# Odd mixer of a fused transformer kernel: unscaled queries, scores of one head per bank, output projection between the head pairs

## The chip, the cores and the metric

The kernel runs on one core of one Trainium2 chip. The metric is the device time of one launch in microseconds (us): 1750.55 us, the median of 3 runs (1749.31 to 1753.45). Lower is better.

## The reference

Two transformer blocks follow each other on a sequence of 256 tokens of width 1024, all in float32. The change lies in the last attention layer, the odd mixer of the second block:

```python
def odd_mixer(x, mix_norm, w_qkv, q_norm, k_norm, w_out):
    proj = rms_norm_2(x, mix_norm) @ w_qkv
    q, k, v = jnp.split(proj, [GQA_Q_WIDTH, GQA_Q_WIDTH + GQA_KV_WIDTH], axis=-1)
    q = rms_norm_2(q.reshape(Bsz, S, 16, 64), q_norm)
    k = rms_norm_2(k.reshape(Bsz, S, 4, 64), k_norm)
    v = v.reshape(Bsz, S, 4, 64)
    q = apply_rope(q, cos, sin)
    k = apply_rope(k, cos, sin)
    return gqa_block_attention(q, k, v) @ w_out
```

There are 16 query heads of 64, each four sharing one key and value head. `rms_norm_2` divides each head's 64 values by the root of their mean square and multiplies by a gain; `apply_rope` turns pairs of values by angles that depend on the position. The attention is softmax over all 256 keys. The block's feed-forward layer (stage f below) follows and ends the kernel.

## The kernel before

Five engine programs are written out by hand: `tensor_program` (PE), `scalar_program` (ACT), `vector_program` (DVE), `gpsimd_program` (POOL) and `sync_program` (SP, which issues the weight loads). Each engine works through its instructions in the written order; semaphores (`on.wait_ge`) tie them together. Ten stages follow each other: a, conv, b, c, attn, d, even, e, odd, f. Here only the last two matter: odd, the mixer above, and f, a feed-forward stage.

Weights come as 260 pieces of 128x2048 in one stream. A piece is split into a high part (ACT copies it to `wh`, 5 slots) and a low part (DVE subtracts, into `wl`, 7 slots), so that three matmuls on reduced-precision operands (`mm3`: high by high, low by high, high by low) give a float32 product. `Ring.fill` and `Ring.need` place these splits in the program of ACT and of DVE; p0 is the first piece of a stage. Stage odd has pieces p0 to p0+9: two for keys and values, four for queries, four for the output projection. A piece is given back for reuse when PE signals `multiplied`.

`tensor_program`'s `odd` projects keys and values (`kv_part(t)`, t the half of 128 tokens), then queries (`q_part(j, t)`, j the half of the heads), 24 matmuls of 512 columns each. DVE scales each head by its root (POOL computes it) and turns it (`rope`); PE transposes (`kv_turn`, `q_turn`). Then the shared function `attention` goes over 8 pairs of heads:

```python
for i in range(n_pairs + 3):
    if i < n_pairs:
        scores(i)
    if 2 <= i < n_pairs + 2:
        turn(i - 2)
    if i >= 3:
        values(i - 3)
    if i in beside:
        beside[i]()
```

`scores(i)` fills two PSUM banks, and a step later can refill them only when ACT's exponentials of that pair are through. DVE first scales the pair before (`scale(i - 1)`: reciprocal of the sums, then four multiplications), then takes the maxima of pair i; ACT makes the exponentials, `turn` transposes the probabilities over two banks, ACT copies them to `PTg`, `values` multiplies by the values, and ACT and DVE split the result into `xTh` and `xTl`. After the last pair, `close` runs the output projection, 96 matmuls of 512 columns: all pieces for t = 0, then all for t = 1, with the transposes for stage f (`turn_in`) ahead of the last piece. `seam` adds the result to x (`post_scale`) and multiplies by the next gain (`pre_scale`) on DVE, squares x on ACT, and places a weight split between.

## Time and profile before

| what | value |
|---|---|
| median of 3 runs | 1750.55 us |
| profiled execution | 1749.03 us, of which the span is 1747.6 us |
| mean granted TensorE clock | 0.975 |
| PE busy | 1664.8 us (95%) |
| DVE busy | 974.7 us (56%) |
| ACT busy | 786.6 us (45%) |
| POOL busy | 69.3 us (4%) |

The span begins with the first instruction and ends with the last; 1.4 us lie outside it. All starts below are us from the span's start. The line numbers are those of the kernel before. PEclk in a window is the granted TensorE clock as a share of 2.4 GHz, so 0.50 is 1.2 GHz and 1.00 is 2.4 GHz.

### The profile page before, as it was taken

Reading aid. Unit: us, or ns where it says so; the run is one execution under the profiler, and the core shown is the slowest. Engines: PE = TensorE matmul, PEld = TensorE weight load, DVE = VectorE, ACT = ScalarE, POOL = GpSimd, SP = SyncE. Lnnn points to the kernel's source line nnn. Section 1 sums busy time; section 2 is a strip of 40 time slices with the busy share of each in tenths; the row PEclk is TensorE's granted clock in tenths of the full one; section 3 lists DMA queues with packets and bytes.
Section 4 is the critical chain, followed back from the end, with each engine's and each line's share of the span. In section 5 each row is a group of like instructions: output and inputs, shape, how many; then the busy total and the mean of one; then the engine's idle time right before and its main releaser. Section 6 shows DMA issues by size and latency. Waiting matters only on the chain. (4 is left out here: it accounts for less than half of the span.)

```text
span 1747.6 us, 18630 instructions
## 1 busy us (share of the span) xinstructions
PE 1664.8 (95%) x7938; PEld 1356.6 (78%) x7938; DVE 974.7 (56%) x992; ACT 786.6 (45%) x954; POOL 69.3 (4%) x99
## 2 busy tenths in 40 slices
PE   6999998999999999999999999988999998599999
PEld 5877776788888888897788889765788886378887
DVE  4646675554565445655545468756454557544543
ACT  5444544443453434554434357534343444534442
POOL 1000000100010000000000000100000002000000
PEclk9999998999999999999999999989999999699999
DMA  8545541454455544553555364313354553026451
GB/s 328 187 179 183 190 159 49 182 200 183 183 192 193 193 168 174 206 193 109 182 182 202 145 229 155 134 43 103 133 217 170 198 189 145 1 99 226 182 192 49
DMA packets 51391, 289.33 MB, mean 166 GB/s; under 512 B 14151, under 2 KB 14791, under 8 KB 18026
## 3 DMA queue, kind: packets, MB, share of 16 engines
q1 hardware_dynamic: 50732, 286.84, 44.9%
q8 instruction: 63, 1.03, 0.2%
q10 hardware_dynamic: 576, 1.29, 0.2%
q14 instruction: 20, 0.16, 0.0%
HBM read 287.06 MB, written 1.05 MB: 165 GB/s over the span
## 5 line engine op out<-in xcount | busy, mean ns | idle before, releaser
L1759 DVE TENSOR_TENSOR wl<-raw,wh 128x2048 fp32r<-128x2048 f32 x260 | 588.7, 2286 | 164.2 <-ACT wh L1145 164.2
L516 PE MATMUL ps<-wh,xTh 128*128 128x512 f32 x1408 | 561.3, 399 | 25.5 <-DVE wl L1759 8.3
L516 PE MATMUL ps<-wh,xTl 128*128 128x512 f32 x1408 | 554.4, 394 | 0.0
L516 PE MATMUL ps<-wl,xTh 128*128 128x512 f32 x1408 | 553.9, 393 | 0.0
L1145 ACT ACTIVATE wh<-raw 128x2048 fp32r<-128x2048 f32 x260 | 489.0, 1908 | 4.2 <-PE ps L516 3.0
L516 PEld LDWEIGHTS ps<-wh,xTh 128*128 128x128 f32 x1408 | 268.0, 190 | 91.4 <-issue 9.8
L516 PEld LDWEIGHTS ps<-wh,xTl 128*128 128x128 f32 x1408 | 267.7, 190 | 57.4
L516 PEld LDWEIGHTS ps<-wl,xTh 128*128 128x128 f32 x1408 | 268.1, 190 | 54.3
L2451 POOL TENSOR_SCALAR st<-st 128x1 f32<-128x1 f32 (+2 forms) x46 | 29.8, 648 | 1490.4 <-ACT tmp L1164 852.4
L1208 ACT ACTIVATE sgf<-ps,st 128x256 f32<-128x256 f32 x22 | 10.4, 474 | 104.1 <-PE ps L516 104.1
L1208 ACT ACTIVATE sge<-ps,st 128x256 f32<-128x256 f32 x22 | 10.4, 474 | 98.9 <-PE ps L516 98.9
L516 PE MATMUL ps<-xTh,wh 128*128 128x256 f32 x192 | 54.6, 284 | 0.0
L516 PE MATMUL ps<-xTl,wh 128*128 128x256 f32 x192 | 54.3, 283 | 0.0
L516 PE MATMUL ps<-xTh,wl 128*128 128x256 f32 x192 | 54.3, 283 | 0.0
L1208 ACT ACTIVATE sgd<-ps,st 128x256 f32<-128x256 f32 x22 | 10.4, 473 | 97.2 <-PE ps L516 97.2
L1208 ACT ACTIVATE sgc<-ps,st 128x256 f32<-128x256 f32 x22 | 10.4, 472 | 95.8 <-PE ps L516 95.8
L1208 ACT ACTIVATE sgb<-ps,st 128x256 f32<-128x256 f32 x22 | 10.4, 472 | 93.0 <-PE ps L516 93.0
L1208 ACT ACTIVATE sga<-ps,st 128x256 f32<-128x256 f32 x22 | 10.4, 474 | 91.7 <-PE ps L516 91.7
L1831 DVE SCALAR_TENSOR_TENSOR hbe<-ps,st,sge 128x256 f32<-128x256 f32 x22 | 10.6, 483 | 73.4 <-ACT sge L1208 73.4
L1831 DVE SCALAR_TENSOR_TENSOR hbf<-ps,st,sgf 128x256 f32<-128x256 f32 x22 | 10.6, 483 | 72.8 <-ACT sgf L1208 72.8
L1831 DVE SCALAR_TENSOR_TENSOR hbd<-ps,st,sgd 128x256 f32<-128x256 f32 x22 | 10.6, 483 | 71.3 <-ACT sgd L1208 71.3
L1831 DVE SCALAR_TENSOR_TENSOR hbc<-ps,st,sgc 128x256 f32<-128x256 f32 x22 | 10.6, 484 | 69.7 <-ACT sgc L1208 69.7
(330 smaller groups left out, 2290.2 us busy)
## 6 DMA issues: line engine op xcount, KB each, us to landing
raw<-in_w SPq DMA_DIRECT2D x260, 1024.0 KB, 4.8
gains<-in_rows SPq DMA_DIRECT2D x18, 512.0 KB, 4.6
x<-in_x ACTq DMA_DIRECT2D x2, 512.0 KB, 7.7
nab<-in_rpb SPq DMA_DIRECT2D x32, 32.0 KB, 2.5
out_x<-x SPq DMA_DIRECT2D x2, 512.0 KB, 2.6
qn<-in_rpb SPq DMA_DIRECT2D x16, 32.0 KB, 2.5
xd<-in_rpb SPq DMA_DIRECT2D x16, 32.0 KB, 2.5
df<-in_cst SPq DMA_DIRECT2D x1, 368.0 KB, 23.4
```

The costliest lines, as they stand in the source:

```text
L516: return pe.matmul(o, lhs, rhs, start=start, stop=stop, skip_group_check=False)
L1145: act.activation(wh[:, p % RING, :], raw[:, p % RAW, :], ACT.Copy).then_inc(*hi(p))
L1208: act.activation(r.sg[:, j % 2, t, :], bank(ffn_bank(j, t))[:, 0:256], ACT.Silu, scale=stat(("r", name, t))).then_inc(*silu(f, j, t))
L1759: TT(wl[:, p % RAW, :], raw[:, p % RAW, :], wh[:, p % RING, :].bitcast(F32), ALU.subtract).then_inc(*lo(p))
L1831: STT(r.hb[:, j % 2, t, :], bank(ffn_bank(j, t))[:, 256:512], stat(("r", name, t)), r.sg[:, j % 2, t, :], ALU.mult, ALU.mult).then_inc(*pr ...
L2451: pool.tensor_scalar(v, ss, mul, add, ALU.mult, ALU.add).then_inc(*mean(*name))
```

## The change

- The queries are no longer scaled by their root. `q_stat` squares them into a buffer of their own (`od.sq`), and `q_rope` turns the raw product straight from PSUM. The root of each head enters later: DVE multiplies the negated maxima with it, and ACT's exponential takes it as its scale.
- The scores are made per head (`scores(i, hh)`), one bank per head (4 and 5), and PE, DVE and ACT go over them head by head. The maxima stand ahead of the scaling of the pair before.
- Probabilities are transposed through one bank (6), half by half, and values use one bank (7).
- The output projection is cut by pair: `out(i, t)` adds 6 matmuls for pair i into banks 0 to 3, and stands between the steps of pair i + 4. The half t = 0 is complete 12 matmuls ahead of the end of t = 1 (before: 48).
- The projections use other banks, and the transposes, copies and weight splits stand elsewhere. On DVE, `turn_in` of the stage's own input comes ahead of the key work.

```diff
+            od.sq = sb("qsq", [128, 512], F32, ph)
...
+        def gqa_root(h):
+            a = 2 * (h % 8)
+            return stat(("r", "qg", h // 8), 16)[:, a:a + 2]
...
+                def scores(i, hh):
+                    on.wait_ge(copied, "kTg", 1)
+                    on.wait_ge(copied, "qTg", i // 4, 1)
+                    clear(4 + hh)
+                    u = slice(64 * hh, 64 * hh + 64)
+                    for t in range(2):
+                        m = mm(bank(4 + hh)[:, 256 * t:256 * t + 256], od.qTg[u, i, 128 * t:128 * t + 128], od.kTg[u, i // 2, :], True, True)
+                    m.then_inc(*scored("gqa", i, hh))
+                    emptied[4 + hh] = [(exped, "gqa", i, hh)]
...
+                def values(i):
+                    clear(7)
+                    for hh in range(2):
+                        for kk in range(2):
+                            on.wait_ge(copied, "gqa", i, kk)
+                            m = mm(bank(7)[64 * hh:64 * hh + 64, 0:256], od.vg[:, kk, 64 * (i // 2):64 * (i // 2) + 64],
+                                   r.PT[:, i % 2, kk, hh, :], kk == 0, kk == 1)
+                    m.then_inc(*valued("gqa", i))
+                    emptied[7] = [(act_lo, "ogqa", i)]
...
+                def out(i, t, mid=None):
+                    p, k = p0 + 6 + i // 2, i % 2
+                    on.wait_ge(act_lo, "ogqa", i)
+                    on.wait_ge(*split_of(p))
+                    if i == 0:
+                        clear(2 * t, 2 * t + 1)
+                    H, L = hi_part(p, 2), lo_part(p, 2)
+                    for half in range(2):
+                        if half and mid:
+                            mid()
+                        u = slice(512 * half, 512 * half + 512)
+                        m = mm3(bank(2 * t + half), xTh[:, i, t, :], xTl[:, i, t, :], H[:, k, u], L[:, k, u], i == 0, i == 7)
+                    if t == 1 and k == 1:
...
+                def keys():
+                    kv_turn(0)
+                    kv_turn(1)
+                    q_turn(0, 0)
 
                 kv_part(0)
-                q_part(0, 0, 5, lambda: turn_in("oddmix", 1))
+                q_part(0, 0, lambda: turn_in("oddmix", 1))
                 kv_part(1)
-                q_part(0, 1, 1)
-                q_part(1, 0, 4, lambda: [kv_turn(t) for t in range(2)])
-                for t in range(2):
-                    q_turn(0, t)
-
-                def q_of(h, t):
-                    on.wait_ge(copied, "qTg", h // 8, t)
-                    return od.qTg[64 * (h % 2):64 * (h % 2) + 64, h // 2, 128 * t:128 * t + 128]
-
-                def k_of(h, n):
-                    on.wait_ge(copied, "kTg", 1)
-                    return od.kTg[64 * (h % 2):64 * (h % 2) + 64, h // 4, 0:n]
-
-                def v_of(h, kk):
-                    on.wait_ge(copied, "vg", 1)
-                    return od.vg[:, kk, 64 * (h // 4):64 * (h // 4) + 64]
-
-                attention("gqa", "odd", 8, 64, [256, 256], q_of, k_of, v_of,
-                          {0: lambda: q_part(1, 1, 7), 3: lambda: [q_turn(1, t) for t in range(2)]})
-                close("odd", "ogqa", 8, None)
+                q_part(0, 1)
+                q_part(1, 0, keys)
+                q_turn(0, 1)
+                scores(0, 0)
+                scores(0, 1)
+                q_part(1, 1, lambda: [scores(1, hh) for hh in range(2)])
+                scores(2, 0)
+                turn(0, 0)
+                scores(2, 1)
+                q_turn(1, 0)
+                turn(0, 1)
+                q_turn(1, 1)
+                for i in range(2, 8):
+                    if i < 7:
+                        scores(i + 1, 0)
+                    turn(i - 1, 0)
+                    if i < 7:
+                        scores(i + 1, 1)
+                    if i >= 4:
+                        out(i - 4, 0)
+                    values(i - 2)
+                    turn(i - 1, 1)
+                    if i >= 4:
+                        out(i - 4, 1)
+                turn(7, 0)
+                out(4, 0)
+                values(6)
+                turn(7, 1)
+                out(4, 1)
+                out(5, 0)
+                values(7)
+                out(5, 1)
+                out(6, 0)
+                out(7, 0)
+                out(6, 1)
+                out(7, 1, lambda: turn_in(AFTER["odd"], 0))
...
+
+                def scores(i, hh):
+                    a, rr = 12 * (i % 3) + 6 * hh, gqa_root(2 * i + hh)
+                    on.wait_ge(peaked, "gqa", i, hh)
+                    if i >= 3:
+                        on.wait_ge(turned, "gqa", i - 3, 1)
+                    for t in range(2):
+                        e = act.activation(r.sc[:, i % 3, t, hh, :], bank(4 + hh)[:, 256 * t:256 * t + 256], ACT.Exp,
+                                           bias=r.sm[:, a + t:a + t + 1], scale=rr[:, t:t + 1], accum_out=r.sm[:, a + 2 + t:a + 3 + t])
+                    e.then_inc(*exped("gqa", i, hh))
...
                 ring.need(p0 + 2)
+                kv_stat(0)
+                ring.fill(1, p0)
                 ring.need(p0 + 4)
                 turn_in("oddmix", 1, free=input_free("e"))
+                q_stat(0, 0)
+                v_copy(0)
                 ring.fill(1, p0)
+                kv_stat(1)
+                q_stat(0, 1)
+                ring.fill(1, p0 + 2)
+                v_copy(1)
                 ring.need(p0 + 6)
+                ring.fill(1, p0 + 2)
+                k_copy(0)
+                k_copy(1)
+                q_turn(0, 0)
+                q_stat(1, 0)
+                q_turn(0, 1)
+                ring.fill(2, p0 + 4)
+                scores(0, 0)
+                scores(0, 1)
+                scores(1, 0)
+                scores(1, 1)
+                q_stat(1, 1)
+                turn(0, 0)
+                scores(2, 0)
+                scores(2, 1)
+                q_turn(1, 0)
+                turn(0, 1)
+                q_turn(1, 1)
+                for i in range(2, 8):
+                    turn(i - 1, 0)
+                    if i < 7:
+                        scores(i + 1, 0)
+                        scores(i + 1, 1)
+                    turn(i - 1, 1)
+                    values(i - 2)
+                    if i == 3:
+                        ring.need(p0 + 10)
+                    if i < 4:
+                        ring.fill(1, p0 + 6)
+                    elif i == 6:
+                        ring.fill(1, p0 + 7)
+                turn(7, 0)
+                values(6)
+                turn(7, 1)
+                ring.fill(1, p0 + 8)
+                values(7)
+                seam("odd", 0, p0 + 8)
+                ring.fill(1, p0 + 9)
+                turn_in(AFTER["odd"], 0, free=(tail, "odd"))
+                seam("odd", 1, p0 + 10)
...
+                def q_rope(j, t):
+                    b = (1, 3, 0, 1)[2 * j + t]
+                    on.wait_ge(squared, "qg", j, t)
+                    rope(0, bank(b).rearrange("p (h d) -> p h d", d=64), 8, t,
+                         [od.qg[:, t, 512 * j:512 * j + 512].rearrange("p (h d) -> p h d", d=64)], "qg", j, t)
+                    head_sum(od.sq[:, :].rearrange("p (h d) -> p h d", d=64), 8, "qg", j, t)
+
+                def scores(i, hh):
+                    a = 12 * (i % 3) + 6 * hh
+                    on.wait_ge(scored, "gqa", i, hh)
+                    dve.tensor_reduce(r.sm[:, a:a + 2], bank(4 + hh).rearrange("p (t n) -> p t n", t=2), AX.X, ALU.max, negate=True).then_inc(*made("peak", i, hh))
+                    on.wait_ge(rstd, "qg", i // 4, 1)
+                    on.wait_ge(made, "peak", i, hh)
+                    TT(r.sm[:, a:a + 2], r.sm[:, a:a + 2], gqa_root(2 * i + hh), ALU.mult).then_inc(*peaked("gqa", i, hh))
+
+                def scale(i):
...
                 ring.need(p0 + 2)
+                ring.fill(1, p0)
+                turn_in("oddmix", 1)
+                tables_of_gains()
+                k_part(0)
                 ring.need(p0 + 4)
+                k_rope(0)
+                q_rope(0, 0)
                 ring.fill(1, p0)
+                k_part(1)
+                q_rope(0, 1)
+                k_rope(1)
+                ring.fill(1, p0 + 2)
                 ring.need(p0 + 6)
+                ring.fill(1, p0 + 2)
+                q_rope(1, 0)
+                ring.fill(2, p0 + 4)
+                scores(0, 0)
+                scores(0, 1)
+                scores(1, 0)
+                scores(1, 1)
+                scale(0)
+                q_rope(1, 1)
+                scores(2, 0)
+                scores(2, 1)
+                scale(1)
+                for i in range(2, 8):
+                    if i < 7:
+                        scores(i + 1, 0)
+                    if i >= 3:
+                        values(i - 3)
+                    if i < 7:
+                        scores(i + 1, 1)
+                    scale(i)
+                    if i == 3:
+                        ring.need(p0 + 10)
+                    if i < 4:
+                        ring.fill(1, p0 + 6)
+                    elif i == 6:
+                        ring.fill(1, p0 + 7)
+                values(5)
+                values(6)
+                ring.fill(1, p0 + 8)
+                values(7)
+                seam("odd", 0, p0 + 8)
+                ring.fill(1, p0 + 9)
+                turn_in(AFTER["odd"], 0)
+                seam("odd", 1, p0 + 10)
```

What the engines now work through, at three places.

DVE, from the last rotation of keys to the first maxima. Before (kd are rotated keys, wl a weight split, r1 and r2 the two halves of a rotation, qg rotated queries, st sums of squares, smg maxima):

```order
L2396 TENSOR_TENSOR kd<-r1,r2 128x4x64 [waits s_made]
L2396 TENSOR_TENSOR kd<-r1,r2 128x4x64
L2082 TENSOR_REDUCE st<-qg 128x8 [waits s_squared]
L1759 TENSOR_TENSOR wl<-raw,wh 128x2048 [waits s_hi]
L2086 TENSOR_TENSOR qg<-ps,st 128x512 [waits s_rstd]
L2392 TENSOR_TENSOR r2<-qg,gcs 128x512 [waits s_made]
L2393 TENSOR_TENSOR r1<-qg,gcs 128x512
L2396 TENSOR_TENSOR qg<-r1,r2 128x512 [waits s_made]
L2082 TENSOR_REDUCE st<-qg 128x8 [waits s_squared]
L2016 TENSOR_REDUCE smg<-ps 128x2 [waits s_scored]
L2016 TENSOR_REDUCE smg<-ps 128x2
```

Now:

```order
L2541 TENSOR_TENSOR kd<-r1,r2 128x4x64 [waits s_made]
L2541 TENSOR_TENSOR kd<-r1,r2 128x4x64
L1897 TENSOR_TENSOR wl<-raw,wh 128x2048 [waits s_hi] x2
L2537 TENSOR_TENSOR r2<-ps,gcs 128x512 [waits s_roped,s_squared]
L2538 TENSOR_TENSOR r1<-ps,gcs 128x512
L2541 TENSOR_TENSOR qg<-r1,r2 128x512 [waits s_made]
L2220 TENSOR_REDUCE st<-qsq 128x8
L1897 TENSOR_TENSOR wl<-raw,wh 128x2048 [waits s_hi] x2
L2564 TENSOR_REDUCE smg<-ps 128x2 [waits s_scored]
L2567 TENSOR_TENSOR smg<-smg,st 128x2 [waits s_made,s_rstd]
```

Between the keys and the first maxima stood the rotation of the queries j = 0, t = 1 and one weight split. That rotation now stands ahead of the keys', and the piece holds the rotation of the queries j = 1, t = 0 with two weight splits on either side, so four where one was.

PE, one step of the pair loop. Before (step i = 6: scores of pair 6, transposes of 4, values of 3):

```order
L516 MATMUL ps<-kTg,qTg 128x256 [waits s_exped]
L516 MATMUL ps<-kTg,qTg 128x256 x3
L770 MATMUL ps<-ident,scg 128x128 [waits s_copied,s_made]
L770 MATMUL ps<-ident,scg 128x128 x3
L770 MATMUL ps<-ident,scg 128x128 [waits s_copied]
L770 MATMUL ps<-ident,scg 128x128 x3
L516 MATMUL ps<-PTg,vg 64x256 [waits s_act_lo]
L516 MATMUL ps<-PTg,vg 64x256 x3
```

Now (step i = 5: scores of pair 6, transposes of 4, values of 3, output projection of pair 1; the rows with wh and wl go on for six matmuls each):

```order
L524 MATMUL ps<-kTg,qTg 128x256 [waits s_exped]
L524 MATMUL ps<-kTg,qTg 128x256
L1108 MATMUL ps<-ident,scg 128x128 [waits s_copied,s_made]
L1108 MATMUL ps<-ident,scg 128x128 x3
L524 MATMUL ps<-kTg,qTg 128x256 [waits s_exped]
L524 MATMUL ps<-kTg,qTg 128x256
L524 MATMUL ps<-wh,xTh 128x512
```

The scores are in two parts, each with its own wait, with the transposes between, and matmuls of the output projection stand behind them.

DVE, from the end of the pairs to stage f. Before:

```order
L2025 TENSOR_TENSOR xTl<-ps,xTh 128x256 [waits s_act_hi] x3
L1784 TENSOR_TENSOR x<-x,ps 128x1024 [waits s_tail]
L1775 TENSOR_TENSOR xn<-x,gains 128x1024 [waits s_flipped,s_added,s_gain_in2]
L1759 TENSOR_TENSOR wl<-raw,wh 128x2048 [waits s_hi]
L1798 TENSOR_TENSOR xTl<-ps,xTh 128x4x128 [waits s_act_hi] x2
```

Now:

```order
L2582 TENSOR_TENSOR xTl<-ps,xTh 128x256 [waits s_act_hi] x2
L1897 TENSOR_TENSOR wl<-raw,wh 128x2048 [waits s_hi]
L2582 TENSOR_TENSOR xTl<-ps,xTh 128x256 [waits s_act_hi]
L1922 TENSOR_TENSOR x<-x,ps 128x1024 [waits s_tail]
L1913 TENSOR_TENSOR xn<-x,gains 128x1024 [waits s_flipped,s_added,s_gain_in2]
L1897 TENSOR_TENSOR wl<-raw,wh 128x2048 [waits s_hi]
L1936 TENSOR_TENSOR xTl<-ps,xTh 128x4x128 [waits s_act_hi] x2
```

The order of the addition (x), the next gain (xn), one weight split (wl) and the input's low part (xTl) is the same; one split more stands ahead of the last pair's xTl.

## Rows read from the trace of the kernel before

**Rows 1.** The page: busy time, share and instructions of each engine.

```profile
PE 1664.8 (95%) x7938; PEld 1356.6 (78%) x7938; DVE 974.7 (56%) x992; ACT 786.6 (45%) x954; POOL 69.3 (4%) x99
```

**Rows 2.** PE timeline, second key and value projection: start, us, what, idle before.

```profile
1451.41 0.80 PE L516 MATMUL ps<-wh,xTh 128*128 128x512 f32 x1 [3.30 <-DVE xTl L1798]
1452.43 0.63 PE L516 MATMUL ps<-wh,xTl 128*128 128x512 f32 x1
1452.86 0.63 PE L516 MATMUL ps<-wh,xTh 128*128 128x512 f32 x1
```

**Rows 3.** PE timeline of the attention pairs and the output projection.

```profile
1472.02 1.46 PE L516 MATMUL ps<-kTg,qTg 64*128 64x256 f32 x8
...
1484.33 1.44 PE L516 MATMUL ps<-kTg,qTg 64*128 64x256 f32 x8 [2.06 <-ACT scg L1363]
...
1499.44 1.94 PE L525 MATMUL ps<-ident,qg 128*128 128x128 f32 x8 [4.87 <-DVE xTl L2025]
...
1506.36 1.13 PE L516 MATMUL ps<-kTg,qTg 64*128 64x256 f32 x8
...
1507.42 1.09 PE L770 MATMUL ps<-ident,scg 128*128 128x128 f32 x8
...
1508.44 1.09 PE L516 MATMUL ps<-PTg,vg 128*64 128x256 f32 x8
...
1533.71 0.50 PE L516 MATMUL ps<-wh,xTh 128*128 128x512 f32 x1 [0.93 <-DVE xTl L2025]
...
1552.93 1.03 PE L525 MATMUL ps<-ident,xn 128*128 128x128 f32 x8
```

**Rows 4.** Windows of 2 us: length, busy by engine, PEclk, DMA share, GB/s.

```profile
1452.00:1454.00 2.00, 2.00 (x6) 1.61 (x5) 0.00 (x0) 0.00 (x0) 1.85 (x2) 0.50 0.00 0
1484.00:1486.00 2.00, 1.44 (x8) 0.69 (x8) 1.68 (x5) 2.00 (x4) 0.34 (x2) 0.76 0.00 0
1502.00:1504.00 2.00, 2.00 (x11) 1.29 (x8) 0.56 (x1) 0.01 (x1) 0.00 (x0) 0.50 0.00 0
```

**Rows 5.** DVE timeline: key rotation, weight split, query rotation, one pair.

```profile
1462.98 0.42 DVE L2086 TENSOR_TENSOR kg<-ps,st 128x256 f32<-128x256 f32 x1
...
1464.23 0.76 DVE L2396 TENSOR_TENSOR kd<-r 128x256 f32<-128x256 f32 x2
...
1466.42 2.29 DVE L1759 TENSOR_TENSOR wl<-raw,wh 128x2048 fp32r<-128x2048 f32 x1 [0.84 <-ACT wh L1145]
...
1469.35 0.69 DVE L2392 TENSOR_TENSOR r<-qg,gcs 128x512 f32<-128x512 f32 x1
...
1507.97 0.42 DVE L2025 TENSOR_TENSOR xTl<-ps,xTh 128x256 fp32r<-128x256 f32 x1 [3.25 <-ACT xTh L1382]
...
1508.50 0.62 DVE L2001 TENSOR_SCALAR scg<-scg,smg 128x256 f32<-128x256 f32 x2
...
1509.76 1.28 DVE L2016 TENSOR_REDUCE smg<-ps 128x2 f32<-128x512 f32 x2
```

**Rows 6.** ACT timeline: a query square, an exponential, two probability copies.

```profile
1470.35 0.60 ACT L1446 ACTIVATE qg<-ps 128x512 f32<-128x512 f32 x1 [2.12 <-PE ps L516]
...
1511.08 0.47 ACT L1363 ACTIVATE scg<-ps,smg 128x256 f32<-128x256 f32 x1 [3.14 <-DVE smg L2016]
...
1512.89 1.09 ACT L1373 ACTIVATE PTg<-ps 128x512 f32<-128x512 f32 x2
```

**Rows 7.** DVE rows, then ACT rows, of the passage to stage f.

```profile
1544.96 1.22 DVE L1784 TENSOR_TENSOR x<-x,ps 128x1024 f32<-128x1024 f32 x1 [11.31 <-PE ps L516]
1546.28 1.23 DVE L1775 TENSOR_TENSOR xn<-x,gains 128x1024 f32<-128x1024 f32 x1
...
1554.19 1.29 DVE L1798 TENSOR_TENSOR xTl<-ps,xTh 128x512 fp32r<-128x512 f32 x2 [2.21 <-ACT xTh L1171]
...
1546.22 1.07 ACT L1158 ACTIVATE tmp<-x 128x1024 f32<-128x1024 f32 x1 [13.02 <-DVE x L1784]
...
1547.74 1.92 ACT L1145 ACTIVATE wh<-raw 128x2048 fp32r<-128x2048 f32 x1 [0.37 <-PE ps L516]
```

163 lines of the change are left out of this document (91 added, 72 removed).

## Prediction

> **What bounds the kernel now.** I read the page first: PE is busy 95% of the span [rows 1], so time goes only where PE waits or runs slowly. The windows of 10 us show such places in stage odd; the engine timelines there give the rest. PE waits 3.30 us before the second key projection [rows 2]. The pairs are a chain: the maxima wait for the scores, the exponentials for the maxima, the transposes for the scaling, and the next scores for the exponentials. PE reaches the first scores at 1472.02 and the output projection at 1533.71 [rows 3]. At full clock one pair costs it about 3.1 us: scores 1.06, transposes 1.02, values 1.03, start to start [rows 3]. Eight pairs are 25 us, the last query projection 5.5 and the late query transposes 0.8, so about 31 of these 61.7 us are work and 30 are waits or half clock. Behind them the output projection is dense: 84 matmuls and more from 1533.71 to the transposes at 1552.93 [rows 3], 0.229 us each, 21.9 us for all 96. After the transposes (0.8) and 12 matmuls, f's first projection starts at **1556.5**. Stage f is dense, so whatever moves this start moves the end alike.
>
> TensorE's clock counts too. After the pause of 3.30 us the matmuls start every 0.43 us [rows 2] with the clock at 0.50 [rows 4], that is 1.2 GHz, against 0.229 at 2.4 GHz: six such matmuls, 1.2 us lost. It also fell around 1485, where PE had paused for 2.06 us and resumed with one set of scores [rows 3, 4], and was still low in 1502 to 1504 though PE had worked since 1499.44 [rows 3, 4]. Transposes of a pair then cost 1.94 instead of 1.09 us [rows 3]. A restart after a pause thus costs 1.2 us at least; held half for 5.8 us it costs 2.9, the upper end I use.
>
> **The change, walked along PE.** I place each step at the latest of what it waits for, at full clock first.
>
> Start. DVE now takes the input's low part ahead of the key work, so the 3.30 us and the six slow matmuls go: 4.6 us gained. The second key projection starts at 1447.9; two and a half projections of 5.45 end at 1461.6. Then the key transposes wait. DVE must first turn the queries j = 0, t = 1, projected at 1459.0: square 0.6 [rows 6], rotation and sum four times 0.61 plus a wait [rows 5], 2.55 in all, and then scale and turn the keys, 2.0 from 1462.98 to 1464.99 in the old trace [rows 5]. Keys are ready at 1464.3. The split of the next piece follows them, 2.2 us [rows 5], so the second half of q_part(1,0) starts at 1466.5 (before 1467.3) and ends at 1469.25. The early gain is nearly all gone. First scores: 1470.65 (before 1472.0).
>
> First pairs. DVE has a rotation (to 1472.7) and two splits (to 1477.1) ahead of the first maxima. Maxima cost 0.68 a head [rows 5] and now a small multiplication, 0.2 with its wait, bounded by nothing and 0.35, a little over half the row of two scalings at 0.62 [rows 5]. An exponential of one head is two of 0.47 [rows 6], 0.9 with the sums. So head 0 of pair 0 is through at 1478.9, and PE, whose half projection ended at 1474.4, gets to the scores of pair 1 only then: 4.5 us idle. The last query projection ends at 1484.65 (it starts slow), the queries' rotation at 1487.5.
>
> Pairs 3 to 5. scores(3,0) at 1489.85, turn(2,0) at 1495.35. Then the two splits inside steps 2 and 3 bite. ACT starts its own behind the copy of values(0), at 1495.6, for 1.9 us [rows 7]; DVE follows with 2.2, then maxima, then the low part of values(0). Bank 7 is the only one for values, so PE waits from 1496.35 to 1501.0 for values(1). In the next step the same wait is 1505.8 to 1509.0. From step 5 on there is no split, and out() of 2.7 us a pair makes PE the bound, 5.8 us a step; DVE needs 3.5 (maxima 1.7, scaling 1.45, low part 0.35). The split of step 6 delays values(5) to 1527.5 (2.3 us idle). The rest of the projection is dense and out(7,0) ends at T = 1541.7.
>
> Passage to f. Before, 48 matmuls (11 us) covered the seam; now 12 do. DVE adds to T + 1.3 and multiplies to T + 2.6 [rows 7]; PE has reached the transposes at T + 1.9 and waits. ACT squares (1.07 and the sum), then splits 1.92 [rows 7], to T + 4.4; DVE's split ends at T + 6.6, the low part of 1.29 [rows 7] at T + 7.9. PE is out of work at T + 4.15. Stage f starts at T + 8.0 = 1549.7. That wait is new: 4.5 us with the small one.
>
> What the queries' missing scaling saves on DVE (four of 0.61) and the 16 small multiplications add (3.2) lie beside PE's work where PE is the bound. In the first pairs they are in the walk. The additional buffer costs nothing; it removes the dependence on the root. POOL's and SP's programs keep their order, and SP's loads of the output pieces have the earlier projections to come in.
>
> Corrections. A first matmul after another kind takes 0.50 instead of 0.39 (the one at 1533.71) [rows 3]; the projection is cut into 16 pieces, so about a dozen more: 1.2 us. Start without clock losses: **1550.9**. Clock: seven places follow waits of 1.5 to 4.6 us. I take 1.8 for the one at 1464 to 1466, 0.9 more than walked for the one at 1479, 0.5 in step 2, 1.2 for values(1) and the transposes behind it (0.9 for each group, partly off the path), 0.3 in step 4, 0.9 for values(5), and 2.2 for f's first matmuls, between 1.2 and 2.9. Sum 7.8, between 4 and 14.4 with each at its end. Result 1550.9 + 7.8 = 1558.7 against 1556.5: **2.2 us later**. The profiled execution took 1749.03, so 1751.2. It lies 1.5 below the median shown; the median's like would be 1752.7.
>
> On the clock the trace says that a restart costs 1.2 us or more [rows 2, 4]. The Trainium skill (TensorE: Matmul & The Clock Gate, "Part 1: The HAM clock gate") says that for modelling the ramp penalty is below 1% of a typical span and a cold count should not be fitted. By this the 7.8 us would be left out and the sum would be that of the first rival. The 7.8 us are indeed below 1% here, but they carry the sign.
>
> **Rivals.** (1) *The clock holds.* PE's pauses are short enough, or the matmuls that wait are off the path, so restarts cost almost nothing: 1550.9, which is 5.6 us earlier, 1743.4. For it: most of the new waits are 2 to 3 us, and PE works between them. Against: the 2.06 us pause at 1482 was enough to lose it [rows 3, 4], and the new waits are longer.
> (2) *The clock stays low through pairs 1 to 5*, slower. Each waiting stretch has only scores, transposes and values in it, and these cost 1.94 instead of 1.09. Then values(1) and values(2), each with its transposes, are 1.8 later, and the first 24 matmuls of out() run at 0.43 instead of 0.229, 4.8 us. Against the 2.0 of steps 2 to 4 in my sum that is 6 us more: 1757. It decides from the point where PE's two waits before values(1) and values(2) come to over 8 us together and out(0,0) does not bring the clock back. For it: rows 1499 to 1504, low for five busy microseconds [rows 3, 4].
> (3) *The change does not do what it says*: the output projection fills no waits, since it starts at step 4, after the long ones. This is largely in my forecast, and has no time of its own.
>
> **How the numbers follow.** A measurement of this kernel can tell about 0.2%, 3.5 us. Forecast with its spread (the clock terms between 5 and 11) 0.45: no change. Rival 1 and waits shorter than walked 0.27: faster. Rival 2 and the passage at its upper end 0.28: slower. The range goes from rival 1, 1743.5, to rival 2 and a little, 1758.
>
> **What the profile would show.** Right: no wait before the second key projection; PE idle near 1462 to 1464, 1474 to 1479, before values(1) and values(2), and 3 to 4 us ahead of f, with a weight split on ACT or DVE just before each; first scores near 1471 to 1473; f's start within 3 us of 1556.5. Wrong: no wait of PE on the low part (xTl) between the pairs; a step without out() shorter than 4 us in pairs 2 to 4; DVE's maxima before 1476; PEclk at 1.00 through the pairs.

## The result and the profile after

After the change the kernel takes **1756.92 us** (median of 8 runs, 1753.75 to 1759.8), beside 1751.32 us (8 runs, 1748.14 to 1753.46) for the kernel before on the same chip: ratio 1.0034, 95% interval 1.0024 to 1.0044. It is slower, by more than the 0.2% that such a measurement can tell. The range held the time, the likeliest case (no change) did not: what came is the time of the second rival, though not quite by its way, as shown below.

The profiled execution took 1757.09 us. The page's busy line, for [rows 1]:

```profile
PE 1683.4 (96%) x7938; PEld 1363.6 (78%) x7938; DVE 974.6 (56%) x1004; ACT 790.9 (45%) x954; POOL 70.7 (4%) x99
```

PE is busy 18.6 us longer with the same 7938 matmuls; DVE has 12 instructions more, the 16 small multiplications less the four large ones, in the same time. A single execution varies by several us from place to place, so below I compare one **stretch**: from the start of the transposes of the oddmix input for t = 1, ahead of the first change, to the start of f's own second input transposes. Before it runs from 1444.31 to 1564.70, 120.4 us; now from 1443.70 to 1572.77, 129.1. Upstream this execution is 0.6 us early, which I add when I set its times beside the forecast's. One window over exactly the stretch, before and then after (columns as in [rows 4]):

```profile
1444.31:1564.70 120.39, 94.78 (x473) 71.62 (x472) 71.73 (x124) 58.32 (x122) 15.28 (x16) 0.86 0.23 88
```

```profile
1443.70:1572.77 129.07, 111.90 (x474) 78.47 (x472) 74.48 (x140) 62.30 (x122) 17.57 (x16) 0.84 0.22 82
```

That is the whole result in two lines. PE's idle time fell from 25.6 to 17.2 us: the change does take waits away, 8.4 us of them. But PE's busy time rose by 17.1 us with the same 472 matmuls (the counts take in one or two that reach over an edge). Together that is the 8.7 us by which the stretch is longer. The mean clock hardly tells (0.86 and 0.84), for it counts idle time too; what matters is what runs while it is low.

PE's timeline (start us, us, engine, line, operation, out and in, count, idle before and what ended it), for [rows 2, 3]:

```profile
1463.64 1.02 PE L533 MATMUL ps<-ident,kd 128*128 128x128 f32 x4 [2.10 <-DVE kd L2541]
...
1470.64 1.14 PE L524 MATMUL ps<-kTg,qTg 64*128 64x256 f32 x8 [0.74 <-ACT qTg L1799]
...
1479.30 3.16 PE L524 MATMUL ps<-kTg,qTg 64*128 64x256 f32 x8 [4.57 <-ACT scg L1807]
...
1491.62 1.13 PE L524 MATMUL ps<-kTg,qTg 64*128 64x256 f32 x4 [1.20 <-ACT scg L1807]
...
1496.21 1.98 PE L524 MATMUL ps<-PTg,vg 128*64 128x256 f32 x8
...
1505.53 1.98 PE L524 MATMUL ps<-PTg,vg 128*64 128x256 f32 x8 [1.24 <-DVE xTl L2582]
...
1516.39 1.98 PE L524 MATMUL ps<-PTg,vg 128*64 128x256 f32 x8
...
1524.59 1.09 PE L524 MATMUL ps<-PTg,vg 128*64 128x256 f32 x8
...
1531.88 1.09 PE L524 MATMUL ps<-PTg,vg 128*64 128x256 f32 x8
...
1538.98 1.98 PE L524 MATMUL ps<-PTg,vg 128*64 128x256 f32 x8 [2.21 <-DVE xTl L2582]
...
1557.78 1.09 PE L533 MATMUL ps<-ident,xn 128*128 128x128 f32 x8 [0.59 <-DVE xn L1913]
...
1562.97 0.79 PE L524 MATMUL ps<-wh,xTh 128*128 128x512 f32 x1 [3.40 <-DVE xTl L1936]
```

The 3.30 us ahead of the second key projection are gone [rows 2]. In their place stand 2.10 and 0.74 us in the start, 4.57 before the scores of pair 1, 1.20 and 1.03 in step 2, 1.24 before values(1), 2.21 before values(5), 0.59 and 3.40 ahead of f. The long waits of the old pair loop are gone too: 2.06, 4.95, 4.87, 3.04, 3.16, 2.46 and 0.93 us, of which [rows 3] shows three. Windows of 2 us (columns as in [rows 4]):

```profile
1478.00:1480.00 2.00, 0.70 (x2) 0.61 (x3) 0.77 (x3) 1.96 (x7) 0.64 (x1) 0.50 0.45 188
1496.00:1498.00 2.00, 2.00 (x9) 0.79 (x8) 1.61 (x6) 0.90 (x5) 0.00 (x0) 0.50 0.00 0
1502.00:1504.00 2.00, 2.00 (x6) 1.17 (x4) 2.00 (x1) 0.60 (x1) 0.00 (x0) 0.50 0.00 0
1510.00:1512.00 2.00, 2.00 (x7) 1.18 (x6) 0.70 (x1) 1.62 (x2) 0.00 (x0) 0.50 0.00 0
1516.00:1518.00 2.00, 2.00 (x10) 0.79 (x8) 0.92 (x4) 0.74 (x4) 0.00 (x0) 0.50 0.00 0
1518.00:1520.00 2.00, 2.00 (x12) 1.47 (x10) 0.00 (x0) 0.87 (x2) 0.00 (x0) 0.90 0.00 0
```

From about 1495 to 1518 the granted clock is 0.50, 1.2 GHz, while PE is busy 2.00 of 2.00 us in nearly every window. Eight value matmuls take 1.98 us there, 1.09 at 1524.59. The eight score matmuls at 1479.30 took 3.16 us, 1.14 at 1470.64; only a part of that is the clock, since eight take 2.08 us at half clock in the kernel before:

```profile
1501.31 2.08 PE L516 MATMUL ps<-kTg,qTg 64*128 64x256 f32 x8
```

The rest of the 3.16 comes from the scores being freed per head: the first of head 1 starts 1.09 us behind the first of head 0, when ACT is through with bank 5. A low clock is nothing new either. One window over the longest part at half clock, before and then after:

```profile
1485.10:1505.60 20.50, 10.68 (x46) 6.90 (x44) 15.60 (x32) 11.38 (x29) 1.83 (x2) 0.50 0.00 0
```

```profile
1494.50:1518.50 24.00, 22.76 (x68) 12.79 (x68) 13.28 (x32) 14.04 (x33) 0.00 (x0) 0.50 0.00 0
```

Over all such parts of the stretch the kernel before spends 34 us at half clock and the changed one 41, but PE is busy in 20.5 of the 34 and in 37.5 of the 41. By an estimate that counts half of this work's time as lost, that is 10.3 us before and 18.8 now: about half of the 17.1. ACT and DVE around the split of a piece inside the pairs, ACT first:

```profile
1500.04 1.91 ACT L1225 ACTIVATE wh<-raw 128x2048 fp32r<-128x2048 f32 x1
```

```profile
1477.06 0.68 DVE L2564 TENSOR_REDUCE smg<-ps 128x2 f32<-128x512 f32 x1
...
1501.98 2.29 DVE L1897 TENSOR_TENSOR wl<-raw,wh 128x2048 fp32r<-128x2048 f32 x1 [3.32 <-ACT wh L1225]
...
1505.06 0.42 DVE L2582 TENSOR_TENSOR xTl<-ps,xTh 128x256 fp32r<-128x256 f32 x1
```

ACT splits for 1.91 us, DVE waits 3.32 us for it and then for the next 2.2 does nothing else; the low part that releases values(1) comes at 1505.06. This is the wait that the forecast named; it is short because PE itself arrives late, only at 1504.3. DVE in the passage to f, for [rows 7]:

```profile
1559.42 2.29 DVE L1897 TENSOR_TENSOR wl<-raw,wh 128x2048 fp32r<-128x2048 f32 x1 [1.70 <-ACT wh L1225]
1561.63 1.28 DVE L1936 TENSOR_TENSOR xTl<-ps,xTh 128x512 fp32r<-128x512 f32 x2
```

The weight split at 1559.42 stands ahead of the low part of f's input (1561.63), and PE waits 3.40 us.

### The profile page after: what moved, and what is told of

The parts are those of the page before. It is cut to its first block, busy times and chain, and to the rows that moved or that the text cites. A ratio compares the mean times of both kernels' runs of the same rounds, so it can differ in the third digit from the quotient of the medians.

```text
span 1755.8 us, 18634 instructions
## 1 busy us (share of the span) xinstructions
PE 1683.4 (96%) x7938; PEld 1363.6 (78%) x7938; DVE 974.6 (56%) x1004; ACT 790.9 (45%) x954; POOL 70.7 (4%) x99
## 3 DMA queue, kind: packets, MB, share of 16 engines
q8 instruction: 63, 1.03, 0.2%
## 4 chain that ended last, share of the span: by engine, by line
PE 88%; DVE 6%; ACT 3%; issue 1%; POOL 1%; DMA 0%; SPq 0%; DVEq 0%; ACTq 0%
PE ps L524 84%; DVE wl L1897 2%; PE ps L623 2%; PE ps L533 1%; ACT wh L1225 1%; PE ps L1108 1%; POOL st L2654 0%; DVE tmp L1928 0%; DVE x L1930 0%; ACT tmp L1244 0%; DMA gains<-in_rows 0%; POOL st L2657 0%; DVE xc L2390 0%; DVE xTl L1936 0%; DVE smn L2393 0%
## 5 line engine op out<-in xcount | busy, mean ns | idle before, releaser
L524 PEld LDWEIGHTS ps<-wh,xTh 128*128 128x128 f32 x1408 | 267.8, 190 | 89.3 <-issue 12.1
L1969 DVE SCALAR_TENSOR_TENSOR hbf<-ps,st,sgf 128x256 f32<-128x256 f32 x22 | 10.6, 483 | 77.1 <-ACT sgf L1288 77.1
L1969 DVE SCALAR_TENSOR_TENSOR hbe<-ps,st,sge 128x256 f32<-128x256 f32 x22 | 10.6, 483 | 73.5 <-ACT sge L1288 73.5
L1969 DVE SCALAR_TENSOR_TENSOR hbd<-ps,st,sgd 128x256 f32<-128x256 f32 x22 | 10.6, 483 | 69.7 <-ACT sgd L1288 69.7
L1969 DVE SCALAR_TENSOR_TENSOR hbc<-ps,st,sgc 128x256 f32<-128x256 f32 x22 | 10.6, 482 | 69.8 <-ACT sgc L1288 69.8
```

The lines of the kernel that those rows point to most:

```text
L524: return pe.matmul(o, lhs, rhs, start=start, stop=stop, skip_group_check=False)
L1969: STT(r.hb[:, j % 2, t, :], bank(ffn_bank(j, t))[:, 256:512], stat(("r", name, t)), r.sg[:, j % 2, t, :], ALU.mult, ALU.mult).then_inc(*pr ...
```

## The experiments

All edits below are to the changed kernel unless said otherwise. Each is timed against the kernel before in the same session (medians 1749.7 to 1750.6); beside its ratio stands the stretch of its one profiled execution.

| kernel | median us (runs) | ratio to before, 95% | stretch us |
|---|---|---|---|
| before | 1751.32 (8) | 1 | 120.4 |
| changed | 1756.92 (8) | 1.0034 (1.0024 to 1.0044) | 129.1 |
| b_warm | 1751.66 (11) | 1.0003 (0.9994 to 1.0012) | 122.0 |
| a_splits_later | 1754.98 (11) | 1.0023 (1.0012 to 1.0034) | 125.4 |
| c_out_behind | 1753.34 (12) | 1.0021 (1.0006 to 1.0035) | 122.5 |
| d_passage | 1752.46 (11) | 1.0011 (1.0003 to 1.0020) | 123.3 |
| g_before_start | 1748.17 (12) | 0.9987 (0.9978 to 0.9996) | 119.3 |
| e_start | 1746.04 (11) | 0.9981 (0.9972 to 0.9990) | 118.5 |
| f_combined | 1728.89 (6) | 0.9894 (0.9876 to 0.9912) | 99.4 |
| h_out_behind | 1735.72 (6) | 0.9918 (0.9896 to 0.9941) | 105.0 |
| l_scale_first | 1736.25 (6) | 0.9921 (0.9896 to 0.9945) | 103.1 |
| m_combined_warm | 1726.33 (5) | 0.9865 (0.9848 to 0.9882) | 98.1 |
| n_scores_together | 1753.97 (9) | 1.0026 (1.0016 to 1.0035) | 124.8 |
| o_combined_together | 1731.22 (4) | 0.9887 (0.9872 to 0.9902) | 105.1 |

Outside the stretch the profiled executions differ by up to 5.7 us (1624.0 to 1629.7), and inside it by 1.9 us where the programs are alike (d_passage and the changed kernel up to values(0)), so a stretch tells small differences only roughly. By their times, b_warm, d, g and e are apart from the changed kernel; the intervals of a, c and n overlap with its own. So do those of h, l and m with f_combined's, and o's with m's: what is said of these rests on their waits, rows and stretch.

**b_warm: is it the clock?** 96 transposes of the identity into a free bank, all but the last 18 in places where PE waits: 32 ahead of scores(1, 0), 8 and 8 in step 2, 30 ahead of values(1), 18 ahead of values(2). They compute nothing.

```diff
+                def busy(b, n):
+                    clear(b)
+                    for _ in range(n):
+                        pe.transpose(bank(b)[:, 0:128], ident[:, :], ident[:, :])
...
+                    if i == 3:
+                        busy(0, 30)
+                    elif i == 4:
+                        busy(2, 18)
```

> From the changed kernel, only PE does more: transposes of the identity into a free bank where it waited (32 before scores(1,0), 8 and 8 in step 2, 30 before values(1), 18 before values(2)), 96 in all. The result does not use them. Theory C (the half clock itself lengthens the pairs): PEclk stays at 1.00 from 1464 on until the passage, and f starts 4 to 7 us earlier than 1563.0 though PE has 12 us more work. Rival W (only the waits count): f starts no earlier, or later by up to 3 us.

Its window over the stretch, one of 2 us inside it, and a PE row:

```profile
1446.70:1568.66 121.96, 110.72 (x569) 82.48 (x568) 74.49 (x140) 61.73 (x122) 17.57 (x16) 0.96 0.24 87
```

```profile
1502.00:1504.00 2.00, 2.00 (x16) 1.64 (x15) 0.95 (x1) 1.51 (x2) 0.00 (x0) 1.00 0.03 8
```

```profile
1502.71 3.50 PE L1145 MATMUL ps<-ident 128*128 128x128 f32 x30
```

The clock is 1.00 from 1488 to 1558; it was still low for about 3.4 us each at 1467, 1484 and 1559, so not from 1464 on as theory C had it. The empty transposes cost 0.117 us each (30 in 3.50), 11 us in all, so about 99.5 of the 110.7 busy us are the kernel's own: 12.4 less than in the changed kernel. PE does more and is through 7.1 us earlier; the kernel is back at the time of before. The low clock is thus a cause, and worth about 0.3% of the time. Of the 4.7 us by which its own busy time still exceeds before's 94.8, more below.

**a_splits_later: the splits inside steps 2 and 3.** Both engines split in steps 4 and 5 instead.

```diff
-                    if i == 3:
-                        ring.need(p0 + 10)
-                    if i < 4:
+                    if i in (4, 5):
```

> From the changed kernel, only the two weight splits at the ends of steps 2 and 3 are moved (on ACT and DVE alike) to the ends of steps 4 and 5. Theory W (the splits make PE wait for the low part of the values, and these waits cost the clock): the waits before values(1) go, the granted clock is not at 0.50 from 1495 to 1518, and stage f starts 5 to 9 us earlier than the 1563.0 of the changed kernel. Rival P (PE is the bound there anyway, since at half clock it is busy nearly all the time): the wait goes but the clock stays low and f starts within 2 us of 1563.

The wait before values(1) is gone and the stretch is 3.7 us shorter, between the 2 us of rival P and the 5 of theory W. The clock still fell and came back at about 1509 instead of 1518. The waits of the start and ahead of f stayed, and 0.55 and 0.70 us came before values(3) and values(4); moved splits alone aren't the cause.

**c_out_behind: without the interleave.** The output projection goes back behind the pairs, its splits with it; all the rest of the change stays.

```diff
-                    if i >= 4:
-                        out(i - 4, 0)
...
+                for t in range(2):
+                    for i in range(8):
+                        if i == 6 and t == 1:
+                            turn_in(AFTER["odd"], 0)
+                        out(i, t)
```

> From the changed kernel, the output projection is put back behind the pairs (all of t = 0, then all of t = 1, with the transposes for f ahead of the last quarter), and the splits with it; the rest of the change stays. Theory I (the interleaving is worth its waits): it takes PE's fill away from steps 4 to 7, each then costs about 3.6 to 4.5 us instead of 6 to 7, and the 22 us of projection follow; the stall of 4 us ahead of f goes. Net f starts 4 to 8 us later than in the changed kernel. Rival S (the loss comes from the seam and the interleaving gives nothing): f starts earlier than 1563 or at the same time.

The rival was right: 122.5 against 129.1 us of stretch, though in an execution 3.1 us below the median of this kernel, and no gain in the time that is clear of noise. The edit takes out two things at once, the interleaving and the short passage to f. Beside d_passage below, which mends the passage and keeps the interleaving (123.3), filling the waits with the projection is worth nothing here. No wait is left ahead of f while the long waits, in the start and in steps 2 and 3, never had any of the projection in them.

**d_passage: the seam.** out(6, 0) moves ahead of values(7) and out(4, 1) behind it, out(5, 1) behind out(7, 0): 12 matmuls instead of 9 stand between the end of t = 0 and f's input transposes, and 6 instead of 3 behind these. ACT and DVE prepare f's input ahead of their split.

```diff
+                turn_in(AFTER["odd"], 0)
+                out(7, 1)
...
-                ring.fill(1, p0 + 9)
                 turn_in(AFTER["odd"], 0)
+                ring.fill(1, p0 + 9)
```

> From the changed kernel, only the passage to stage f: out(4,1), out(5,1), out(6,1) stand behind or beside out(7,0), so that three pieces of 6 matmuls lie between the end of t = 0 and the transposes where it was one and a half, and on ACT and DVE the transposed input comes ahead of the weight split. Theory: the waits of 0.59 and 3.40 us ahead of f shrink to under 0.7 together, and f's first matmuls run at full clock (1.2 to 2.9 us): f starts and goes on 4 to 6 us earlier, the run is 4 to 6 us faster than the changed kernel. Rival: the split, now later, holds up the second gate projection of f by what was gained, and the time is within 1.5 us.

(In the program that ran it is two pieces of 6 matmuls, not three.)

```profile
1557.36 1.09 PE L533 MATMUL ps<-ident,xn 128*128 128x128 f32 x8
...
1560.03 0.49 PE L524 MATMUL ps<-wh,xTh 128*128 128x512 f32 x1 [0.18 <-DVE xTl L1937]
```

The waits of 0.59 and 3.40 become 0 and 0.18, f's first matmul takes 0.49 instead of 0.79 us, and the stretch is 5.7 shorter. From values(5) on, where the edit lies, it is 26.9 instead of 33.8 us; ahead of that this execution ran 1.1 us longer with the same program. The passage is a real part of the loss.

**g_before_start and e_start: the start.** g is the kernel before with one thing of the change: the input's low part ahead of the key work on ACT and DVE. e is the changed kernel with ACT's and DVE's work up to pair 1 in the order in which PE needs it:

```diff
                 k_part(1)
+                ring.fill(1, p0 + 2)
+                k_rope(1)
                 q_rope(0, 1)
-                k_rope(1)
-                ring.fill(1, p0 + 2)
-                ring.need(p0 + 6)
-                ring.fill(1, p0 + 2)
-                q_rope(1, 0)
-                ring.fill(2, p0 + 4)
+                ring.fill(1, p0 + 3)
                 scores(0, 0)
                 scores(0, 1)
+                q_rope(1, 0)
...
```

> The kernel before with one part of the change alone: DVE's and ACT's share of the input's second half comes ahead of the key work. Theory (the gain of 4.6 us at the start is lost again at once, because the keys and queries are rotated no sooner): PE's wait of 3.30 us goes, others of together 2.5 to 4 us come before the key or query transposes, and the run is within 1.5 us of the kernel before. Rival (it is a real part that the rest of the change gives back): 3.5 to 4.6 us faster than before.

> From the changed kernel, only the order on ACT and DVE up to pair 1: the split of the second query piece and of the first output piece stand ahead of the late keys, the keys are turned ahead of the queries j = 0, t = 1, the first maxima stand ahead of the queries j = 1, t = 0, and the third output piece is split behind the scaling of pair 0. PE's order is the same. Theory S (the first maxima are 6 to 10 us late because of two rotations and four splits ahead of them): first exponentials at 1467 to 1470 where they were at 1478.0, PE's waits of 2.10 and 4.57 us gone, and the stretch from one input transpose to the next (129.1 us in the changed kernel, 120.4 before) is 8 to 11 us shorter. Rival L (the lead is lost again at the splits of steps 2 and 3 and in a clock that falls all the same): under 5 us shorter.

```profile
1465.23 0.65 PE L525 MATMUL ps<-ident,kd 128*128 128x128 f32 x4 [1.14 <-DVE kd L2403]
...
1471.32 0.66 PE L525 MATMUL ps<-ident,qg 128*128 128x128 f32 x4 [2.25 <-DVE qg L2403]
```

```profile
1459.62 0.66 PE L533 MATMUL ps<-ident,kd 128*128 128x128 f32 x4 [0.59 <-DVE kd L2540]
...
1464.63 1.14 PE L524 MATMUL ps<-kTg,qTg 64*128 64x256 f32 x8 [0.74 <-ACT qTg L1799]
```

In g the 3.30 us are gone and 1.14 and 2.25 have come: of 3.3 us 1.1 are kept in the stretch, and 0.13% in the time (1.7 us of the median, where 1.5 at most were expected). That the gain of the start is lost to what follows on DVE is a matter of its order, since in e the waits are 0.59 and 0.74, the 4.57 before pair 1 is gone (0.35 and 1.97 stand in the first steps), and the stretch is 10.6 us shorter than the changed kernel's. But the clock still fell, 1482 to 1506.

**f_combined: all the cures together.** e's start, d's seam, ACT's splits in steps 4 to 7, DVE's in steps 5 to 7 behind the scaling, and one more behind values(5). The cut shows DVE's loop.

```diff
-                    if i == 3:
-                        ring.need(p0 + 10)
-                    if i < 4:
+                    if 5 <= i:
                         ring.fill(1, p0 + 6)
```

> e_start and d_passage together, and the splits in steps 4 to 7 only, on DVE one step later than on ACT and behind the scaling, so that no low part of the values waits for one. Theory: waits gone, PE dense from the first scores but for about 0.5 us a step in steps 2 and 3, the clock at 1.00; PE's work from the first scores to f is 54 us, so the stretch is 102 to 108 us where the changed kernel had 129.1 and the kernel before 120.4: 12 to 18 us (0.7 to 1.0%) faster than before. Rival: a pair's chain over three engines is longer than the 3.6 us of DVE's share, so steps 2 and 3 last 5 us or more each and the clock falls: 110 to 115 us.

```profile
1482.17 1.13 PE L524 MATMUL ps<-kTg,qTg 64*128 64x256 f32 x4 [1.20 <-ACT scg L1808]
...
1505.18 1.09 PE L524 MATMUL ps<-PTg,vg 128*64 128x256 f32 x8
...
1512.47 1.09 PE L524 MATMUL ps<-PTg,vg 128*64 128x256 f32 x8
...
1535.92 0.51 PE L524 MATMUL ps<-wh,xTh 128*128 128x512 f32 x1 [0.17 <-DVE xTl L1933]
```

PE waits twice in step 2 (1.20 and 1.03) and then not again until 0.17 us ahead of f; a step with the projection takes 7.29 (1505.18 to 1512.47). The stretch is 29.7 us shorter than the changed kernel's and 21.0 shorter than before's, and shorter than the 102 to 108 expected. That is 9.7 more than the parts alone add up to (3.7, 5.7 and 10.6). About 7 of these are idle time: 13.3 us of it are gone, where the three parts together took away 6.4. The wait before values(5) is among them; a, d and e all still had it (2.35, 2.20, 2.20). The other 3 are busy time. The clock is at half for 3.4 us, against 27 to 31 in each part.

**h_out_behind, l_scale_first: two parts of the change, in a kernel whose pairs are hardly held up.** h is f_combined with the output projection behind the pairs; l is f_combined with the pair before scaled ahead of the next maxima on DVE, as the kernel before does.

```diff
+                    scale(i)
                     if i < 7:
                         scores(i + 1, 0)
...
-                    scale(i)
```

> The combined kernel (stretch 99.4 us) with its output projection put back behind the pairs and the passage of the kernel before. Theory (interleaving pays only where the pairs' chain is not held up otherwise): steps 4 to 7 become bound by DVE and the chain at 3.6 to 4.5 us, PE idles 0.5 to 1.4 us in each and may lose the clock, the projection of 22 us follows: 6 to 12 us more than the combined kernel, still 6 us or more faster than before. Rival (as in the changed kernel, where c_out_behind was no slower): within 2 us of the combined kernel.

> The combined kernel with DVE's scaling of a pair ahead of the maxima of the next one, as it was before the change. Theory (the maxima ahead of the scaling let ACT's exponentials start 1.45 us sooner, which counts only where PE waits, in the steps ahead of the output projection): 1 to 4 us slower than the combined kernel. Rival (DVE has the same work in any order and is the bound there): within 1 us.

The interleave is worth 5.5 us of stretch here (6 to 12 were expected) and nothing in c: here it fills waits that are short and many (h has eight of 0.3 to 1.3 us). The maxima first are worth 3.7 us of stretch, a clock at half for 6.8 instead of 3.4 us included; without them a wait of 3.42 stands before a pair's scores:

```profile
1485.30 1.24 PE L524 MATMUL ps<-kTg,qTg 64*128 64x256 f32 x4 [3.42 <-ACT scg L1808]
```

**m_combined_warm.** f_combined with 8 and 8 of the empty transposes in step 2's two waits.

> The combined kernel with 8 and 8 transposes of the identity in PE's two waits of step 2 (1.20 and 1.03 us), after which the clock fell from 1485 to 1489. Theory C: the clock stays at 1.00 and the stretch is 1 to 2 us shorter than 99.4, the time 1 to 2 us lower. Rival: the clock falls with or without them, and the time is equal within 0.5 us or higher.

The clock stays at 1.00 through the whole stretch: 98.1 us, 1726.33, the lowest median of all, 1.35% below before (interval 1.18 to 1.52%). The last 1.4 us of stretch go with the clock, as theory C had it; the time alone can't tell them from noise.

**n_scores_together, o_combined_together: the overlap of two heads.** The rows of steps 4 to 6 did not fit my sum: from values(2) to values(5) three steps of 8.2, 7.3 and 7.1 us (1516.39, 1524.59, 1531.88, 1538.98 above), where I had 5.8. In the first of them values(2) still ran at half clock, and the third has the wait of 2.21 in it, so 7.3 is the price of a step at full clock. Counting matmuls shows why. At 1470.64 eight score matmuls, both heads, take 1.14 us, as eight did before (the row of 1506.36 in [rows 3]); where a transpose stands between the heads, four of one head take 1.13. n issues both heads behind turn(i - 1, 0); o does so in m_combined_warm.

```diff
-                    if i < 7:
-                        scores(i + 1, 0)
                     turn(i - 1, 0)
                     if i < 7:
+                        scores(i + 1, 0)
                         scores(i + 1, 1)
```

> The changed kernel with the two heads' scores of a pair issued one behind the other, behind turn(i - 1, 0) instead of around it. In the trace of the changed kernel four score matmuls of one head alone take 1.13 us (1.06 to the next start), and eight of both heads together 1.14 us at 1470.64, as eight of before did: the two heads lie on different halves of the rows and run beside each other only where nothing stands between them. Theory P (the lost overlap is a price of the change that my sum left out): every pair's scores come back to one row of 1.14; in the three steps where PE is the bound (7.1 to 7.3 us, values to values) the step falls to about 6.2, and in the half-clock steps by up to 2. The stretch from the input transposes to f's own falls from 129.1 to 121 to 125, the time to 1750 to 1753. Rival W (PE waits anyway): in the steps the 1.06 us turn into waits for the exponentials, which now must be through for both heads, only the last steps gain, and the stretch stays within 3 us, 126 to 129.

> m_combined_warm with the two heads' scores together. There PE is busy without a gap from 1486 to f and a step takes 7.27 us, so theory P has five steps shorter by 1.06: the stretch falls from 98.1 to 92.5 to 94.5, the time to about 1721. Rival W: ACT, which needs about 5.7 us in a step with a split, or the chain maxima, exponential, scores becomes the bound of a step of 6.2; then new waits on scg or xTl of 0.3 to 1 us each appear and the stretch stays above 95.5.

```profile
1494.80 0.63 PE L1108 MATMUL ps<-ident,scg 128*128 128x128 f32 x4 [4.13 <-ACT PTg L1814]
...
1516.25 1.09 PE L524 MATMUL ps<-PTg,vg 128*64 128x256 f32 x8
...
1519.68 1.14 PE L524 MATMUL ps<-kTg,qTg 64*128 64x256 f32 x8
...
1522.34 1.09 PE L524 MATMUL ps<-PTg,vg 128*64 128x256 f32 x8
...
1528.45 1.09 PE L524 MATMUL ps<-PTg,vg 128*64 128x256 f32 x8
```

```profile
1484.61 0.63 PE L1108 MATMUL ps<-ident,scg 128*128 128x128 f32 x4 [3.25 <-ACT PTg L1824]
...
1492.27 0.85 PE L1108 MATMUL ps<-ident,scg 128*128 128x128 f32 x4 [1.90 <-ACT PTg L1824]
...
1496.52 1.98 PE L524 MATMUL ps<-PTg,vg 128*64 128x256 f32 x8 [1.37 <-DVE xTl L2587]
```

In n the steps are 6.1 us (1516.25, 1522.34, 1528.45) instead of 7.3: theory P holds where PE is the bound. From values(2) to values(5) n needs 3.3 us less; about 0.9 of them are the clock, low at the changed kernel's values(2) and not at n's. Over the stretch it is 4.3, and the time, 1753.97, just misses the 1750 to 1753 expected. PE's busy time fell by 11.2 us, but its idle time rose by 7.0: the early steps got something like rival W, 4.13 us in one place, though the wait is for copies and not for exponentials. PE stands at turn(1, 0) until ACT has copied the transposes before, with the scores queued behind it. In o this decides: three waits of 3.25, 1.90 and 1.37 us, the clock at half from 1486 to 1489 and from 1492.5 to 1506, and 7.1 us of stretch lost, though its late steps are 6.1 too. (The profiled execution was the slowest of the four; the medians are 4.9 us apart.) So by these rows scores apart are right in the early steps and wrong in the steps with the projection. A kernel with the heads apart up to step 3 and together from step 4 was not run; by these rows it should gain about 3 us on m_combined_warm, which stays a guess.

## Why the prediction was right in part and missed the size

- **The start** was right. Forecast: keys ready 1464.3, first scores 1470.65, scores of pair 1 at 1478.9, scores(3, 0) at 1489.85, all without the 2.7 to 3.2 us of clock. Measured, with the 0.6: 1464.2, 1471.25, 1479.9 and 1492.2, so 2.4 late at the last. Of the 4.6 us gained ahead of the second key projection 0.8 are left at the first scores (1.35 as walked), and g and e show the reason, DVE's order.
- **Waits before values(1) and values(2)**: the mechanism was right, the split in front of the low part (1501.98, 1505.06; without it, in a_splits_later, the wait is gone), but not what it would look like. Forecast 4.65 and 3.2 us of idle PE; measured 1.24 and none, because PE was late itself. values(1) started 5.1 us later than walked at full clock, values(2) 8.0.
- **The clock** is the first term that was mis-sized. The sum had 7.8 us for it, 2.0 of them for steps 2 to 4; I took each loss as a restart after a pause, of 1.2 to 2.9 us, which ends when work comes. It did not end from 1495 to 1518: PE was busy 22.8 us at half clock there, about 11.4 us lost by estimate (half of them), of which shorter waits before values(1) and values(2) took back a part. The kernel before already showed this. Its clock is at 0.50 from 1485.1 to 1505.6 and from 1519.1 to 1529.3, and the forecast used only the windows around 1485 and 1502. The second rival described it, and its time came, in part by luck. Its decision point was wrong: PE's two waits came to 1.24 together, not to the "over 8 us" that it asked for. And most of its price, 4.8 us, was for the first 24 matmuls of out() at half clock, while only the six of out(0, 0), just ahead of values(2) at 1516.39, ran so; the clock came back at 1518.5. Holding the clock in b_warm gave 7.1 us. Why it stays low so long here is open: in f_combined the same two waits of step 2 (1.20 and 1.03) cost 3.4 us of half clock and not 24. The Trainium skill (TensorE: Matmul & The Clock Gate, "Part 1: The HAM clock gate"), by which no cold count should be fitted, would have given the first rival and the wrong sign. Here the clock is the difference between 1.0003 and 1.0034: less than 1%, as the page says, but all of the loss.
- **The steps with the projection** are the second: a term that the sum left out. "scores 1.06" was read from a row of eight matmuls in which two heads overlap, and carried over to a program that issues them apart. Each pair from 2 to 7 pays 1.06 us more at full clock; between values(2), 8.0 late, and values(5), 12.1 late, two pairs' scores stand, so of the 4.1 us that came on there 2.1 to 2.4 are the lost overlap (n's steps are 1.2 shorter).
- **The passage** was right: forecast 0.7 and 3.85 us of waits with f starting slow; measured 0.59 and 3.40, 0.79 for the first matmul.
- **The sum**: 1558.7 against 1556.5, 2.2 us later, counted f's slow first matmuls in. Against it stands the stretch, which has them too: 8.7 us longer, so 6.5 more than forecast. f's first projection itself started at 1563.6 (with the 0.6), 7.1 behind before's, not within 3. The lost overlap and a clock low for longer than allotted are of a size to cover it; how they share the part at half clock, where longer scores are also slower ones, the runs don't separate.
- **The extra instructions** that I hid beside PE (16 small multiplications of 0.16 us each on DVE) left DVE's total unchanged. Where PE waits for the first exponentials they are on the path, 0.3 us from the end of the first maxima (1477.74) to the exponential (1478.04), as the walk had it; that they are hidden elsewhere was not tested. The first maxima came at 1477.06, 1477.7 with the 0.6, where I had walked them to 1477.1.
- **The third rival**, that the projection fills no waits, is true of the changed kernel (c beside d) and was rightly part of the forecast and not a time of its own.

## What to carry to other kernels

When an edit moves work between others, look at each row's count before using its time again: a duration of grouped matmuls belongs to the order in which they were issued. A wait removed on PE is worth what the next thing in the queue of DVE or ACT allows, so order those queues by when PE needs each result, and put bulk work such as weight splits where PE has a row of dense matmuls. And a low clock need not end when the waits do: ask how much work stands in the stretch that already runs at half clock, since moving work into it costs double (20.5 us of work there before, 37.5 after). Single cures showed little each (3.7, 5.7, 10.6 us), and all together far more (29.7).

## What the runs showed of the hardware

- The clock can stay at 0.50 for 24 us while the profile has PE busy for 22.8 of them; empty transposes in and between the waits held it at 1.00 (b_warm over these steps, m_combined_warm over the whole stretch). What decides how long it stays low, the runs don't show.
- Score matmuls with 64 rows of contraction, of two heads on different halves of the rows, run beside each other (8 in 1.14 us) when they are issued together; with a pair's transposes between the heads, 4 take 1.13.
- An exponential whose scale is a column of a tile was slower than one without, on the same 128x256 of PSUM. Each row is a group (count, shortest/median/longest ns, first and last start), after and before:

```profile
L1807 ACT ACTIVATE scg<-ps,smg,st x32: 553/560/566, 1478.0 to 1531.9; 128x256 f32<-128x256 f32 x32
```

```profile
L1363 ACT ACTIVATE scg<-ps,smg x32: 463/472/479, 1475.8 to 1525.1; 128x256 f32<-128x256 f32 x32
```

That is 88 ns each, 2.8 us of ACT for 32. By the order of the rows they lie beside PE's work, except in the first pairs; no run tested it.
